# K and Q rotated by VectorE out of PSUM, in place of products with a permutation

## The reference, cut to what matters

```python
proj = h @ w_in
z, xbc, dt_raw, q, k, v, g = jnp.split(proj, offs, axis=-1)

def rotary(x, pos):
    half = x.shape[-1] // 2
    ...
    x1, x2 = x[..., :half], x[..., half:]
    return jnp.concatenate([x1 * cos - x2 * sin, x1 * sin + x2 * cos], axis=-1)

q = rotary(q.reshape(b, L, RET_HEADS, RET_QK_DIM), pos)
k = rotary(k.reshape(b, L, RET_HEADS, RET_QK_DIM), pos) * (RET_QK_DIM ** -0.5)
```

## Time and profile before

| | us |
|---|---|
| median of 3 runs | 1720.81 (1719.25 to 1721.04) |
| the profiled execution: its own time | 1720.76 |
| the profiled execution: its span | 1718.9 |
| TensorE busy (matmuls) | 1618.8, 94% of the span |
| VectorE busy | 534.5, 31% |
| ScalarE busy | 298.8, 17% |
| mean DMA rate | 223 GB/s |

### The profile page before, as it was taken

One profiled execution on the slowest core, in us unless ns is written; L12 is line 12 of the kernel. 1 busy time (PEld: TensorE's weight loads), 2 busy tenths in 40 slices (PEclk: granted clock), 3 DMA queues, 4 the chain that ended last, 5 costly groups with the idle time before them and its releaser, 6 DMA issues.

```text
span 1718.9 us, 20388 instructions
## 1 busy us (share of the span) xinstructions
PE 1618.8 (94%) x8728; PEld 1010.3 (59%) x8728; DVE 534.5 (31%) x1094; ACT 298.8 (17%) x634; POOL 14.2 (1%) x30
## 2 busy tenths in 40 slices
PE   7999999889998999999999999997999899999996
PEld 4776668567765654444377675684676565445442
DVE  2024664551142311211210275645312222211122
ACT  1013322130121210001101142212202112001002
POOL 0000000000000000000000000000000000000000
PEclk9999999899999999999999999999999999999998
DMA  7223212764266399999922231237544735999993
GB/s 282 109 99 147 102 50 95 297 255 161 98 267 256 123 396 365 379 389 369 391 93 105 104 142 54 99 140 302 220 147 162 295 149 233 368 387 378 364 379 152
DMA packets 28685, 382.54 MB, mean 223 GB/s; under 512 B 3184, under 2 KB 3568, under 8 KB 3888
## 3 DMA queue, kind: packets, MB, share of 16 engines
q1 hardware_dynamic: 25040, 356.49, 53.1%
q0 software_dynamic: 3552, 24.71, 3.6%
HBM read 356.48 MB, written 24.71 MB: 222 GB/s over the span
## 4 chain that ended last, share of the span: by engine, by line
PE 84%; DMA 8%; DVE 3%; ACT 3%; DVEq 1%; issue 1%; ACTq 0%; SPq 0%; POOL 0%; POOLq 0%
PE psum L515 33%; PE psum L1084 13%; PE psum L881 8%; PE psum L1104 6%; PE psum L1069 6%; PE psum L1129 5%; DMA st_out<-states_out 4%; DMA ring<-stream 4%; PE psum L531 1%; PE psum L640 1%; PE psum L960 1%; PE psum L500 1%; PE psum L728 1%; PE psum L978 1%; PE psum L528 1%
## 5 line engine op out<-in xcount | busy, mean ns | idle before, releaser
L515 PE MATMUL psum<-h,ring 128*128 128x320 f32 x1664 | 463.3, 437 | 3.4 <-DMA ring<-stream 2.5
L515 PEld LDWEIGHTS psum<-h,ring 128*128 128x128 f32 x1664 | 316.9, 192 | 141.5 <-issue 11.8
L1084 PE MATMUL psum<-ring,work 128*64 128x512 f32 x1024 | 232.0, 597 | 1.2 <-DMA ring<-stream 1.2
L1084 PEld LDWEIGHTS psum<-ring,work 128*64 128x64 f32 x1024 | 69.6, 137 | 136.9 <-issue 130.0
L881 PE MATMUL psum<-work,ring 128*128 128x320 f32 x512 | 139.7, 433 | 0.9 <-ACT work L1251 0.9
L515 PE MATMUL psum<-mem,ring 128*128 128x256 f32 x512 | 124.4, 398 | 7.9 <-DMA ring<-stream 4.0
L1104 PE MATMUL psum<-ring,work 128*64 128x512 f32 x512 | 115.1, 602 | 7.2 <-ACT work L1491 7.2
L881 PEld LDWEIGHTS psum<-work,ring 128*128 128x128 f32 x512 | 96.5, 190 | 40.7 <-ACT work L1251 1.8
L515 PEld LDWEIGHTS psum<-mem,ring 128*128 128x128 f32 x512 | 99.8, 199 | 31.6 <-issue 12.6
L1069 PEld LDWEIGHTS psum<-work 128*128 128x128 f32 x768 | 92.7, 200 | 25.1 <-issue 25.1
L1069 PE MATMUL psum<-work 128*128 128x128 f32 x768 | 98.3, 287 | 2.2 <-DVE work L2010 2.2
(11 more groups left out here) (273 smaller groups left out, 1299.7 us busy)
## 6 DMA issues: line engine op xcount, KB each, us to landing
ring<-stream SPq DMA_DIRECT2D x168, 2048.0 KB, 9.6
st_out<-states_out POOLq DMA_DIRECT2D x18, 1024.0 KB, 10.2
mk_out<-k_mem POOLq DMA_DIRECT2D x2, 1024.0 KB, 7.8
mv_out<-work POOLq DMA_DIRECT2D x2, 1024.0 KB, 5.6
x<-x_in SPq DMA_DIRECT2D x1, 1280.0 KB, 5.9
y_out<-h POOLq DMA_DIRECT2D x2, 640.0 KB, 3.2
cst<-consts SPq DMA_DIRECT2D x1, 1270.0 KB, 22.0
mem<-mem_in SPq DMA_DIRECT2D x1, 1024.0 KB, 23.9
```

What stands on the lines that cost most here:

```text
L515: mm = pe.matmul(out, w[:, a:a + P], rhs[:, j, :], start=(j == 0), stop=(j == KD - 1))
L1084: mm = pe.matmul(psum[ab * CAP:(ab + 1) * CAP, up, :], h_packed[:, p % 2, k, ab * CAP:(ab + 1) * CAP], w[:, a:a + BANK], start=(k == 0), s ...
```

## The change

TensorE no longer multiplies K and Q with `rot`, and the constant is gone (64 KB of the second load). ScalarE no longer copies the K and Q chunks. VectorE takes them out of PSUM itself, in three products and a sum: the sum's first term for partitions 0 to 63 is read from partitions 64 to 127 of the bank and the other way round, and written to the opposite half of `rot_tmp`. The table of sines carries the sign, its lower half as it was and its upper half negated; each product reads the half of the table that lies on the partitions of its PSUM operand. The bank's release for K and Q is now counted by VectorE (`s_vout`, which goes to 16 a layer), and ScalarE's count per layer falls from 37 to 29. VectorE rotates a chunk as soon as its projection is done, where it did so behind the XBC chunk of the same number before. TensorE's wait for the tables stands behind the first two Z chunks.

```diff
@@ consts
-          ("rot", P), ("cos", T), ("sin", T), ("causal", P), ("causal_s", LG),
+          ("cos", T), ("sin", T), ("causal", P), ("causal_s", LG),
-FIRST = CAT["rot"]
+FIRST = CAT["cos"]
-    put("sin", np.tile(np.sin(ang), (2, 1)))
+    put("sin", np.concatenate([np.sin(ang), -np.sin(ang)], 0))
@@ TensorE
                 def evacuated(n):
-                    if n < KD:
-                        pe.wait_ge(s_vout, L * KD + n + 1)
+                    if n < 2 * KD:
+                        pe.wait_ge(s_vout, L * 2 * KD + n + 1)
                     else:
-                        pe.wait_ge(s_evac, L * 37 + n - KD + 1)
+                        pe.wait_ge(s_evac, L * 29 + n - 2 * KD + 1)
...
                 project(Q_K, range(4))
                 project(Q_Q, range(4))
-                pe.wait_ge(s_tables, 16)
-                for j in range(12):
-                    project(Q_XBC, [j])
-                    if j < 2 * RH:
-
-                        pe.wait_ge(s_evac, L * 37 + j + 1)
-                        if j >= 2:
-                            pe.wait_ge(s_rotated, L * 8 + j - 1)
-                        pe.matmul(psum[:, 4 + j % 2, 0:T], k_("rot", P), kq[:, j, :], start=True, stop=True)\
-                            .then_inc(s_rot, 1)
+                project(Q_XBC, range(12))
...
                 project(Q_Z, range(2))
                 pe.wait_ge(s_rotated, (L + 1) * 8)
+                pe.wait_ge(s_tables, 16)
@@ ScalarE
-                n_evac = KD
+                n_evac = 2 * KD
-                for c in range(8):
-                    evac(kq[:, c, :])
@@ VectorE
                 dve.wait_ge(s_tables, 16)
+                half = DK // 2
+                sin = k_("sin", T)
                 for j in range(2 * RH):
-                    dve.wait_ge(s_rot, L * 8 + j + 1)
+                    dve.wait_ge(s_proj, L * 45 + KD + j + 1)
                     tmp = rot_tmp[:, j % 2, :]
-                    dve.tensor_tensor(tmp, psum[:, 4 + j % 2, 0:T], k_("sin", T), ALU.mult)
-                    dve.tensor_tensor(kq[:, j, :], kq[:, j, :], k_("cos", T), ALU.mult)
+                    own = psum[:, (KD + j) % 4, 0:T]
+                    dve.tensor_tensor(tmp[0:half], own[half:P], sin[half:P], ALU.mult)
+                    dve.tensor_tensor(tmp[half:P], own[0:half], sin[0:half], ALU.mult)
+                    dve.tensor_tensor(kq[:, j, :], own, k_("cos", T), ALU.mult).then_inc(s_vout, 1)
                     dve.drain()
                     dve.tensor_tensor(kq[:, j, :], kq[:, j, :], tmp, ALU.add).then_inc(s_rotated, 1)
```

More of the change, by code:

```diff
@@ L114, in constants @@
     half = DK // 2
[L115 to L119, removed]
     pos = np.concatenate([np.arange(SEQ), np.tile(PAST + np.arange(DS), DB)]).astype(np.float32)
@@ L294, in build @@
         s_evac = sem("s_evac")
-        s_rot = sem("s_rot")
         s_rotated = sem("s_rotated")
@@ L705, in mixer @@
                             pe.wait_ge(s_mem, 16)
-                            pe.wait_ge(s_evac, (L + 1) * 37)
+                            pe.wait_ge(s_evac, (L + 1) * 29)
                             turn_late(2)
@@ L1589, in mixer @@
                 d = [dt_tmp[0:H, i, :] for i in range(6)]
-                dve.wait_ge(s_evac, L * 37 + 21)
+                dve.wait_ge(s_evac, L * 29 + 13)
                 dve.tensor_scalar(d[0], d[0], par[0:H, L, PAT["dt_bias"]:PAT["dt_bias"] + 1], None, ALU.add)
@@ L1619, in mixer @@
                 for c in range(CC):
-                    dve.wait_ge(s_evac, L * 37 + 8 + c + 1)
+                    dve.wait_ge(s_evac, L * 29 + c + 1)
                     if c >= 2:
@@ L1663, in mixer @@
                     dve.wait_ge(s_tout[i % 2], turned_by(L, i))
-                dve.wait_ge(s_evac, L * 37 + 29)
+                dve.wait_ge(s_evac, L * 29 + 21)
                 def head_rows_of(step):
@@ L1779, in mixer @@
                 add_skip(9)
-                dve.wait_ge(s_evac, (L + 1) * 37)
+                dve.wait_ge(s_evac, (L + 1) * 29)
                 for t in range(3):
```

## The result

| | kernel before | changed kernel |
|---|---|---|
| median of the first 7 runs each, us | 1720.81 (1715.03 to 1722.78) | 1705.13 (1703.27 to 1713.08) |
| ratio of the changed to the before | | 0.9922, 95% interval 0.9901 to 0.9944 |
| the profiled execution: its time, its span | 1720.76, 1718.9 | 1705.48, 1703.6 |
| mean of the executions of the study | 1720.75 (106 executions) | 1706.96 (19 executions) |

The 19 take in the first seven of the changed kernel; the 106 are those run beside the experiments, and with the first seven of the kernel before their mean would be 1720.67. One execution of the run a_back8 (2458 us at a mean granted clock of 0.64) was slow and is left out everywhere.

What follows compares the result with a forecast made beforehand. TensorE, busy for 94% of the span, was taken as the bound. Removing 16 x 0.538 = 8.61 us, all else nothing, gave a span of 1710.3, plus 1.9 around it: 1712.2 us, range 1708.6 to 1716.0.

Steps and rivals of the forecast that it cites:

- The products leave TensorE: K/Q rotation among the XBC chunks: 16 products of 0.538 us each leave the chain, 8.61 us gained.
- What is late next in that stretch: XBC chunks: with the products gone nothing else delays TensorE, chunks run back to back at 4.31 us; cost nothing.
- last sign of being wrong: End of layer 0: the prediction is wrong if the lead of 4.3 us is gone before layer 1 begins.
- VectorE's four instructions: K/Q chunks: three products and a sum take 1.86 us, at most 2.14, against TensorE's 4.31; cost nothing.
- third rival: K/Q bank release: VectorE falls behind TensorE if half products take 2.2 us; at 3.0 the time is 1738; chance 0.02.
- The rotation moves ahead: Before the XBC chunks: VectorE rotates earlier, then fills the conv tile and waits for dt as now; costs nothing.
- the tables: Second load of constants: lands 22.0 us after 3.7 us, VectorE needs it at 58.5 us; nothing.
- ScalarE's copies: K/Q chunks: 16 copies of 0.44 us, 7.0 us, leave an idling engine, not on the chain; nothing.
- Behind the stretch: Rest of each layer: weight loads move with TensorE, so the whole gain passes through, 4.30 us a layer.
- second rival: Experts' stage: the weight stream sets the time and swallows the gain, anything up to 1720.8 us; chance 0.03.
- clock rival: Gate chunks after short matmuls: TensorE's slow clock falls elsewhere, giving 1718.2, 1716.2 or, as a gain, 1708.2; chance 0.10.
- How sharp that is: Whole program: equal work in both layers drifts by up to 3 us, so the forecast's own range is about 3 us either way.

Runs made afterwards that it cites:

- a_back8: The changed kernel with one idle TensorE product put back behind each of the first eight XBC chunks of each layer: 1717.7 +- 0.9 us.
- 8 + 8: The changed kernel with eight idle TensorE products put back in each layer, two runs together: 11.9 us over the base.
- b_noprod: The kernel before without its sixteen products and TensorE's waits before them; VectorE's rotation reads the copied chunk itself, late as before: 1709.0 +- 0.6 us.
- the base: The changed kernel's executions pooled with those of the changed kernel with 128 unused constant columns where `rot` stood: 1707.0 +- 0.7 us (25 executions).

## Why the prediction was wrong, step by step

- **The products leave TensorE: right, to the hundredth.** 0.538 us each was forecast, 8.61 in all; both layers show 4.31 us less. 64 idle products at 34.4 us of own time cost 35.2, 34.7 and 35.7 in three places.
- **What is late next in that stretch: right.** Nothing; 27 chunks run back to back. The prediction's last sign of being wrong, a lead that is gone before layer 1, did not come: in the first profiles the 4.3 us had grown to (865.79 - 24.00) - (859.51 - 24.78) = 7.1.
- **VectorE's four instructions: right.** 2.08 us a chunk, between the forecast 1.86 and the bound of 2.14; a half product 0.49. Its starts are 0.51, 0.49 and 0.59 us apart, where the pair of whole products before stood 0.41 apart: the halves don't overlap their forerunner. The Trainium skill, "VectorE: DVE Perf Modes", Two Vector instructions with no wait between them, says just that of instructions that change their start quadrant; this trace agrees, at about 0.1 us each. That all three read PSUM now isn't the reason: four products with a sum on line 1795, each with a PSUM operand and all from partition 0, run back to back in 1.41 us at 0.41 each, so they start 0.33 apart and do overlap.

```profile
288.09 1.41 DVE L1795 SCALAR_TENSOR_TENSOR states_out<-states_out,psum 128x256 f32<-128x256 f32 x4 [6.86 <-PE psum L745]
```

  The third rival needed 2.2 us for a half product and fell with the 0.49.
- **The rotation moves ahead, the tables, ScalarE's copies: costless, as said; whether they gained is open.** The kernel before is 1.9 +- 0.8 us slower than the changed one with 8 + 8 products (1720.75 against 1718.86), and b_noprod 2.0 +- 1.6 slower than the base. The forecast had zero. The first is little over two standard errors, the second little over one. The one place that fits is the wait in layer 1's states, 5.3 and 4.3 us in the two profiles of the kernel before, and 3.5 and 3.3 in those of 8 + 8; b_noprod, with the old copies and the late rotation, has 3.4 there, which speaks against it.
- **"Behind the stretch. I let the whole gain through": this step failed.** I took the rest of the program for something that moves rigidly with TensorE, and put its own change at nothing. On average it became 5.1 +- 0.8 us shorter: 3.2 +- 1.0 with the products' going and 1.9 from the last point. Of the stages that were shorter in the first profiles only the states of layer 1 are so in all six profiles of the two kernels, by 0.6 us at least. That the rest depends on how far layer 0 is moved is shown (9.2 us at 17, 0.7 at 34), and about 1.2 of the 9.2 are one wait for weights; where the others come from, and why the kernel before lies on the dear side, is open. The second rival, that the weights would swallow the gain, fell the other way.
- **The clock rival names a part of it and had too small a say.** It named slow stretches that fall elsewhere, as a loss or as a gain down to 1708.2, at 0.10. The withheld time fell from 39.2 to 36.5 us on average, up to 2.7 of the 5.1.
- **"How sharp that is" failed too.** I took 3 us from one profile's two layers and a before that was shown with three runs 1.8 us apart. Single executions have a standard deviation of 3.4 us, so a median of seven is uncertain by some 1.6, and a difference of two by over 2, before any mechanism. Two such errors, 4.6 us, would have made the range 1707.6 to 1716.8 around the same forecast. That holds the mean of 1707.0 almost, and the first median of 1705.13 still not.

## What to carry to other kernels

Time that comes off the engine that bounds a stretch is read from the chain: the period with the work, less the period without (0.538 us a product here, borne out in three places). What the rest of the program does with an earlier start is not zero, and here was more than half as much again; where later stages idle TensorE beside DMA traffic, give it several us of range on both sides. Profile a kernel more than once before naming the stages of a small difference: two of the three that the first pair showed did not come again. Measure with idle work put back in one place at a time before calling an extra a price: idle work spread over two layers looked like a price per product, and was none.

## What the runs showed of the hardware

- VectorE's product on 64 partitions that reads one half of PSUM and writes the other half of SBUF takes 0.48 to 0.49 us for 320 columns, as one on 128 partitions does.
- Products that change their start half don't overlap the one before (0.50 us from start to start, not 0.41: about 0.1 us each); products with a PSUM operand that don't change it do (0.33 us apart at 0.41 each).
- The same program takes 1711.9 to 1730.6 us, at a mean granted clock of 0.971 to 0.983.
- 32 idle products in layer 0 cost 26.5 us, 64 there 35.2, and 32 in layer 1 18.7. With the 32 in layer 0 one wait for weights is 2.4 us long, with the 64 it is 1.2.
